# Seven products for the input duos alone, and the root on the output tiles

## The chip, the core and the metric

The kernel runs on one core of a Trainium2 chip. The metric is the time of one execution in microseconds (us) on the device. The engines are TensorE (PE; its weight loads are PEld), VectorE (DVE), ScalarE (ACT), GpSimd (POOL) and SyncE (SP, which issues most DMAs).

## What is computed

One layer of a hybrid encoder for 592 tokens (64 sample, 16 meta, 512 prompt) of width 1024: a feed-forward half-step, a combined projection with a state-space branch and an attention branch, their merge, and a second feed-forward half-step. The change concerns the two half-steps alone:

```python
def rmsnorm(x, g):
    xf = x.astype(jnp.float32)
    y = xf * lax.rsqrt(jnp.mean(xf * xf, axis=-1, keepdims=True) + EPS)
    return (y * g.astype(jnp.float32)).astype(x.dtype)

def swiglu(x, w_in, w_out):            # w_in 1024 x 5632, w_out 2816 x 1024
    a, b = jnp.split(x @ w_in, 2, axis=-1)
    return (jax.nn.silu(a) * b) @ w_out

h = h + 0.5 * swiglu(rmsnorm(h, norm_ffn1), ffn1_w_in, ffn1_w_out)
... the mixer ...
h = h + 0.5 * swiglu(rmsnorm(h, norm_ffn2), ffn2_w_in, ffn2_w_out)
```

## The kernel before

**Precision.** Every product of fp32 matrices is made of three matmuls in fp32r: each operand is split into a high part (rounded, an ACT copy) and a low part (the rest, a DVE subtraction), and high x high, low x high and high x low are summed in PSUM. So every weight tile costs ACT one pass and DVE one pass. `wh` and `wl` hold the parts of two slots of weights, 2048 elements per partition each; `raw` holds what the DMA brought, also two slots.

**Duos.** A feed-forward block (`ffn`, called with e = 0 and 1; 592 tokens, then 576) is a list of 38 duos, made by `duos_of`. An *input duo* makes one tile of 128 hidden features: two column tiles of w_in (a and b) times 1024 rows. An *output duo* adds two column tiles of 128 outputs to h. The 22 hidden tiles come in four parts of 6, 6, 6 and 4 (`PARTS`); in each part the input duos are followed by four output duos that sum over the part's tiles. Duo q uses PSUM banks 0 to 3 or 4 to 7 by turns.

**Seven products.** A duo is a product of a 2 x 2 block matrix of weights (two column tiles, two halves of the rows) and one of tokens (two halves of the rows, two halves of the tokens). A plain duo makes the eight block products, one half of the tokens in each matmul: 96 matmuls for an input duo. A *fast* duo (`fast`) makes seven by sums of blocks (Winograd's form of Strassen's product): 84 matmuls for input, 63 for an output duo of six tiles. Before, all input duos but the first of a block are fast and so are the twelve output duos of parts 0 to 2; the four output duos of the last part are plain, with 48 matmuls each.

**What a fast duo needs beside PE.** Four sums of weight blocks, all by POOL (`sum_for`, L904), written into `wl` in place of the low parts to come; six batches of high copies by ACT (`upper`, L1232) and six of low subtractions by DVE (`lower`, L1756), since the seven products need seven weight operands of 512 elements; four snapshots of partial sums from PSUM by ACT (`snap`, L1258); the sums of token blocks. The latter are made once per block for the input duos (`input_sums`, `input_upper`, `input_lower`), but for every hidden tile for the output duos (`first_difference`, the `late` tiles, `hidden_upper`, `hidden_lower`, L1270 to L1295, L1797 to L1820).

**Root.** The norm's root `rs` (one value per token) multiplies the a tile in `gate_a` (DVE) and, for b, the silu's result in two POOL operations (L952). In `gate_b` DVE adds and multiplies in four operations of half the tokens. After a fast output duo POOL adds two snapshots to h (L939, L944), and DVE adds the PSUM banks (`add_pair`).

**Order.** Every engine runs its instructions in the order of its list; the loops over duos interleave by hand what belongs to duo q, to the one before and to the one after. On ACT, for an input duo: snapshot 0, second hidden copy of the previous duo, weights of places 4 and then 0 of the next, snapshots 1 and 2, weights of places 1 to 5, silu, snapshot 3, first hidden copy (L1270 in the last part), last weights. In the first block the sum of squares (`square`, `gather`, `sum_squares`, `root`, `inverse`) runs beside duos 0 and 1, and the DMA of a slot is issued when `split_done` says that the slot's last low part is made.

## Time and profile before

| | us |
|---|---|
| median of 3 runs | 2122.32 (2121.72 to 2122.92) |
| profiled execution | 2123.01 |
| its span | 2121.3 |
| PE busy in it | 1930.2 (91%) |
| DVE, POOL, ACT busy | 1393.8, 1071.1, 1066.9 |
| first block, first matmul to last | 17 to 509 |
| second block | 1634 to 2103 |

Times in rows are us from the start of the span. Busy time of PE is a union of overlapping matmuls: a matmul's own duration (some 0.30 us) is longer than the distance to the next (0.14 us), so a stage is read by its length and the number of its matmuls. "PEclk" is the granted clock of PE, 1.00 being 2.4 GHz and 0.50 being 1.2 GHz. In a timeline "[1.62 <-DVE full]" is idle time of the engine before the row, and what ended it.

### The profile page before, as it was taken

What the parts mean: (1) busy time and instruction counts of PE and PEld (TensorE: products, weight loads), DVE (VectorE), ACT (ScalarE), POOL (GpSimd) and SP (SyncE); (2) the same over time, 40 slices, a digit from 0 to 9 for tenths busy, and PEclk for the clock granted to TensorE, in tenths of its full rate; (3) what the DMA queues carried; (4) which work ended last, traced back from release to release, by engine and by line L of the source; (5) the groups of instructions that cost most, each with busy time, mean ns of one, the idle gap of its engine ahead of it and who ended that gap; (6) DMA issues with size and microseconds to landing.
All of it is one profiled execution on the core that took longest, in us unless ns stands there. A gap on an engine that the chain in (4) does not pass through costs nothing. (4 is left out here: it accounts for less than half of the span.)

```text
span 2121.3 us, 37219 instructions
## 1 busy us (share of the span) xinstructions
PE 1930.2 (91%) x14087; PEld 1856.7 (88%) x14087; DVE 1393.8 (66%) x2151; ACT 1066.9 (50%) x2271; POOL 1071.1 (50%) x1024
## 2 busy tenths in 40 slices
PE   5788798889899999999999999999999789888787
PEld 4778798789799999999999999999999778888787
DVE  5898989877765356346635661224555898989874
ACT  5545545445565556555655664442224545545444
POOL 5578686852464345425432642232112578687760
PEclk9899999999899999999999999999999999999999
DMA  4212232224322412522161225234342113222222
GB/s 109 60 60 81 70 90 75 65 80 131 90 83 83 148 56 89 164 76 77 58 199 41 84 83 153 68 119 136 113 125 80 48 58 95 70 85 75 71 70 75
DMA packets 226959, 190.61 MB, mean 90 GB/s; under 512 B 11136, under 2 KB 215232, under 8 KB 225632
## 3 DMA queue, kind: packets, MB, share of 16 engines
q1 hardware_dynamic: 221824, 173.76, 26.9%
q0 software_dynamic: 4416, 14.32, 2.2%
q8 instruction: 112, 1.84, 0.4%
q14 instruction: 63, 0.52, 0.1%
q10 hardware_dynamic: 544, 0.17, 0.0%
HBM read 168.89 MB, written 19.33 MB: 89 GB/s over the span
## 5 line engine op out<-in xcount | busy, mean ns | idle before, releaser
L1040 POOL TENSOR_TENSOR wl<-raw,wh 128x512 fp32r<-128x512 f32 (+1 forms) x184 | 232.5, 1271 | 407.3 <-ACT wh L1163 406.9
L2189 PE MATMUL ps<-xah,wh 128*128 128x296 f32 (+1 forms) x1376 | 308.6, 306 | 11.9 <-DVE xal L1687 7.4
L2189 PE MATMUL ps<-xah,wl 128*128 128x296 f32 (+1 forms) x1376 | 307.8, 305 | 0.0
L2189 PE MATMUL ps<-xal,wh 128*128 128x296 f32 (+1 forms) x1376 | 302.3, 301 | 0.0
L1756 DVE TENSOR_TENSOR wl<-wl_plain,wh 128x512 fp32r<-128x512 f32 (+3 forms) x198 | 253.1, 1305 | 49.4 <-POOL wl_plain L904 26.7
L1232 ACT ACTIVATE wh<-wl_plain 128x512 fp32r<-128x512 f32 (+3 forms) x198 | 142.7, 721 | 196.3 <-POOL wl_plain L904 182.9
L2189 PEld LDWEIGHTS ps<-xah,wh 128*128 128x128 f32 x1376 | 223.0, 191 | 13.9 <-DVE xal L1687 6.4
L2189 PEld LDWEIGHTS ps<-xal,wh 128*128 128x128 f32 x1376 | 224.0, 190 | 0.0
L2189 PEld LDWEIGHTS ps<-xah,wl 128*128 128x128 f32 x1376 | 222.7, 190 | 0.1
L904 POOL TENSOR_TENSOR wl_plain<-raw 128x512 f32<-128x512 f32 (+1 forms) x132 | 187.1, 1425 | 12.6 <-PE ps L2256 12.0
L2256 PE MATMUL ps<-xth,wh 128*128 128x296 f32 (+1 forms) x504 | 156.3, 310 | 37.5 <-ACT act L1258 28.9
L2256 PE MATMUL ps<-xah,wh 128*128 128x296 f32 (+1 forms) x516 | 157.9, 306 | 33.0 <-ACT full L1258 17.8
L1756 DVE TENSOR_TENSOR wl<-raw,wh 128x512 fp32r<-128x512 f32 (+1 forms) x198 | 182.1, 937 | 0.2 <-DVE ss L1698 0.2
L952 POOL TENSOR_TENSOR act<-act,rs 128x296 f32<-128x296 f32 (+1 forms) x84 | 91.1, 1104 | 128.9 <-ACT act L1262 128.9
L2256 PE MATMUL ps<-xal,wh 128*128 128x296 f32 (+1 forms) x516 | 155.7, 302 | 0.0
L2256 PE MATMUL ps<-xah,wl 128*128 128x296 f32 (+1 forms) x516 | 155.6, 302 | 0.0
L2256 PE MATMUL ps<-xth,wl 128*128 128x296 f32 (+1 forms) x504 | 152.7, 303 | 0.0
L2256 PE MATMUL ps<-xtl,wh 128*128 128x296 f32 (+1 forms) x504 | 151.8, 301 | 0.0
L2256 PEld LDWEIGHTS ps<-xth,wh 128*128 128x128 f32 x504 | 97.7, 194 | 46.2 <-issue 35.7
L2256 PEld LDWEIGHTS ps<-xah,wh 128*128 128x128 f32 x516 | 99.6, 193 | 39.3 <-issue 29.6
L2201 PE MATMUL ps<-wh,xal 128*128 128x256 f32 (+1 forms) x440 | 128.0, 291 | 0.0
L2201 PE MATMUL ps<-wh,xah 128*128 128x256 f32 (+1 forms) x440 | 125.6, 286 | 1.1 <-ACT zr L1457 1.1
(394 smaller groups left out, 5559.5 us busy)
## 6 DMA issues: line engine op xcount, KB each, us to landing
raw<-in_ffn_w_in_dram SPq DMA_DIRECT2D x88, 512.0 KB, 5.1
raw<-in_w_in_dram SPq DMA_DIRECT2D x80, 512.0 KB, 4.5
raw<-in_ffn_w_out_dram SPq DMA_DIRECT2D x48, 384.0 KB, 3.7
brow<-acs_rows SPq DMA_DIRECT2D x8, 1184.0 KB, 6.7
raw<-in_w_br_ssm_dram SPq DMA_DIRECT2D x16, 512.0 KB, 3.9
bias<-bias_rows SPq DMA_DIRECT2D x32, 160.0 KB, 4.6
os_spill<-yT SPq DMA_DIRECT2D x8, 592.0 KB, 3.0
bias<-biasp_rows SPq DMA_DIRECT2D x16, 264.0 KB, 5.6
```

The source lines that it names most:

```text
L904: ins = pool.tensor_tensor(place(p, hk), a, b, op)
L952: pool.tensor_tensor(a, a, halfway(G["rs"][:, :], t, half), ALU.mult).then_inc(scaled_ready, 1)
L1040: ins = pool.tensor_tensor(wl[:, slot, k, 0:cols], raw[:, slot, k, 0:cols], wh[:, slot, k, 0:cols].bitcast(F32), ALU.subtract)
L1232: act.activation(places(wh, p, n, hk), src, ACT.Copy).then_inc(hi_ready if c == 5 else wh_part, 1)
L1756: dve.tensor_tensor(places(wl, p, n, hk), src, places(wh, p, n, hk).bitcast(F32), ALU.subtract)\
L2189: ins = pe.matmul(bank(b + a, half), w[:, slot, k, j * P:(j + 1) * P], x[:, k, a * half:(a + 1) * half], start=(k == 0 and w is wh and x i ...
L2201: ins = pe.matmul(bank(b, 256, m), x[:, k, t * P:t * P + m], w[:, slot, k, :], start=(k == 0 and w is wh and x is xh), stop=(k == KT - 1 a ...
L2256: ins = pe.matmul(bank(duo.b + b, half), weights_of(w, p, k), operand(duo, name, k, low), start=(start and k == 0 and w is wh and low == 0 ...
```

## The change

- `PRODUCTS` serve input duos alone. All output duos are plain (72 matmuls in parts 0 to 2, 48 in the last). In the first block two input duos are plain, in the second one (`PLAIN_IN`).
- The blocks of the rows are now every second row tile (tile 2k and tile 2k+1) instead of the lower and the upper four; T4 is a fourth tile in `xth` and `xtl` instead of overwriting x.
- Three of the four weight sums lie in a buffer of their own (`sums`), the fourth in `raw` in place. POOL makes the first and the one in place, DVE the two others (`sum_2`, `sum_4`). POOL's work in a block is these two sums per fast duo and no more; it starts them after the sum of squares is ready.
- The weights of a fast duo are split in three batches of 1024, 1536 and 1024 elements (`upper_x`, `upper_y`, `upper_z` and the same `lower_`), instead of six.
- An output duo's weights are one batch (`upper_plain`, `lower_plain`), at 0 or at 2560 in the row of `wh`.
- The root no longer multiplies b: `gate_b` is two operations on all tokens, POOL's two multiplications are gone, and the output tiles are multiplied by `rs` in `add_out`, ahead of the addition to h.
- Hidden tiles are kept as they are: one high copy, one low subtraction.
- The orders on ACT and DVE are new; in the second block the low halves of the token sums are made while w_out's product runs.

```diff
-PLAIN = len(PARTS) - 1
-HALF_IN, HALF_OUT = 4, 3
-FAST, FAST_OUTS = 33, 12
+PLAIN_IN = (2, 1)
@@ duos_of
-                fast = len(out) > 0 if into else part != PLAIN
+                fast = into and len(out) >= PLAIN_IN[ffn]
@@
-PRODUCTS = ((0, "B11", 3, True, 1), (1, "T1", 1, True, 2), (2, "T2", 3, False, 2), (3, "B22", 1, False, 3),
-            (4, "B21", 0, True, 4), (5, "T3", 3, False, 5), (6, "T4", 2, True, None))
+PRODUCTS = ((0, "B11", 3, True), (1, "B21", 0, True), (2, "T1", 1, True), (3, "T2", 3, False),
+            (4, "B22", 1, False), (5, "T3", 3, False), (6, "T4", 2, True))
@@ POOL: all of ffn (sums, additions into h, differences, multiplications by the root) becomes
+                pool.wait_ge(ss_ready, (1, 3)[e])
...
+                    pool.wait_ge(raw_ready[slot], raw_loads(duo, slots))
+                    pool.wait_ge(wl_part, 2 * duo.d)
+                    pool.tensor_tensor(G["sums"][:, 0, :].rearrange("p (k c) -> p k c", k=4), chunk(slot, 2, 1), chunk(slot, 2, 2), ALU.add)\
+                        .then_inc(s1_made, 1)
+                    pool.wait_ge(s2_made, duo.d + 1)
+                    pool.tensor_tensor(chunk(slot, 2, 1), chunk(slot, 1, 1), chunk(slot, 2, 1), ALU.subtract).then_inc(s3_made, 1)
@@ ACT, in the loop over duos
+                    if duo.fast:
+                        upper_z(duo)
+                        snap(duo, 0)
+                        if prev.into:
+                            hidden_upper(prev)
+                        if after.fast:
+                            upper_x(after)
+                        snap(duo, 1)
+                        if not after.fast:
+                            upper_plain(after)
+                        snap(duo, 2)
+                        if after.fast:
+                            upper_y(after)
+                        silu(duo)
+                        snap(duo, 3)
...
@@ DVE
+                def gate_b(duo):
+                    a, b = in_halves(actb[:, duo.s, :]), in_halves(full[:, duo.s, :])
+                    if duo.fast:
+                        dve.wait_ge(snap_ready, 4 * duo.d + 4)
+                        dve.wait_ge(prod_done, 7 * duo.d + 7)
+                        dve.tensor_tensor(b, halves(duo.b + 2, half=half), b, ALU.add).then_inc(c_done, 1)
+                        dve.wait_ge(c_done, duo.d + 1)
+                        dve.wait_ge(gated, duo.i + 1)
+                        dve.tensor_tensor(b, b, a, ALU.mult).then_inc(hid_made, 1)
...
+                def add_out(duo, u):
+
+                    hm, scaled = G["h"][:, 2 * duo.n + u, :], actb[:, u, :]
+                    dve.wait_ge(lin_out, unit_out(duo, u))
+                    link(dve.tensor_tensor(in_halves(scaled), halves(duo.b + 2 * u, half=half), rs, ALU.mult))
+                    dve.scalar_tensor_tensor(out=hm, in0=scaled, scalar=0.5, in1=hm, op0=ALU.mult, op1=ALU.add).then_inc(dve_free, 1)
...
+                    if duo.fast:
+                        if prev.into:
+                            gate_b(prev)
+                        lower_z(duo)
+                        if after.fast:
+                            sum_2(after)
+                        if prev.into:
+                            hidden_lower(prev)
+                        if after.fast:
+                            lower_x(after)
+                            sum_4(after)
+                        else:
+                            lower_plain(after)
+                        gate_a(duo)
+                        if after.fast:
+                            lower_y(after)
@@ DVE, opening of the first block
-                if m >= 4:
-                    input_sums(0, m - 4)
+                if m % 2:
+                    input_sums(0, m // 2)
+                if m in (4, 6):
+                    input_lower(0, m // 2 - 2)
@@ PE, in fast
+                        if p in (0, 2):
+                            pe.wait_ge(wl_part, 2 * duo.d + (1 if p == 0 else 2))
+                        if p == 5:
+                            duo_split()
...
+                        if not start:
+                            pe.wait_ge(snap_ready, 4 * duo.d + {3: 1, 4: 2, 5: 3}[p])
@@ PE
-            ffn(0, F1, (1, 1, 0), opening)
+            ffn(0, F1, (1, 0, 12, 0), opening)
...
-            ffn(1, G2, (0, 2, 4), closing=first_turns)
+            ffn(1, G2, (0, 1, 2, 4), closing=first_turns)
```

## Rows read from the trace of the kernel before

**Rows 1.** The page: busy time by engine, and the load of an input duo

```profile
PE 1930.2 (91%) x14087; PEld 1856.7 (88%) x14087; DVE 1393.8 (66%) x2151; ACT 1066.9 (50%) x2271; POOL 1071.1 (50%) x1024
...
raw<-in_ffn_w_in_dram SPq DMA_DIRECT2D x88, 512.0 KB, 5.1
```

**Rows 2.** Busy time by stage, the whole core (x is the number of instructions)

```profile
core 0: us, PE busy (x) PEld busy (x) DVE busy (x) ACT busy (x) POOL busy (x), PEclk, DMA share, GB/s
...
202.00:215.37 13.37, 11.95 (x87) 11.58 (x85) 12.14 (x15) 7.16 (x14) 9.63 (x8) 1.00 0.31 89
...
257.16:273.33 16.17, 10.76 (x66) 10.31 (x64) 14.66 (x19) 7.61 (x17) 11.66 (x11) 0.79 0.18 59
...
273.33:282.79 9.46, 8.81 (x66) 8.60 (x64) 7.57 (x9) 4.71 (x10) 8.56 (x8) 1.00 0.27 85
...
441.03:454.39 13.36, 11.69 (x86) 11.48 (x85) 11.11 (x14) 6.61 (x12) 7.62 (x7) 1.00 0.28 80
...
489.26:495.85 6.59, 6.59 (x51) 6.59 (x50) 4.66 (x6) 3.53 (x5) 0.00 (x0) 1.00 0.17 31
...
2082.66:2089.06 6.40, 6.40 (x51) 6.40 (x49) 3.32 (x4) 2.32 (x3) 0.00 (x0) 1.00 0.01 4
...
73.36:509.15 435.79, 378.50 (x2630) 366.99 (x2631) 378.79 (x429) 217.02 (x430) 302.48 (x238) 0.97 0.26 75
...
509.15:1634.01 1124.86, 1105.22 (x8363) 1058.95 (x8362) 563.56 (x1208) 570.23 (x1303) 423.04 (x487) 0.99 0.33 103
...
1669.94:2103.11 433.17, 370.32 (x2642) 358.48 (x2641) 374.24 (x422) 212.86 (x426) 297.84 (x238) 0.98 0.24 71
```

**Rows 3.** Waits of PE, 73 to 509 us: total us, times, longest

```profile
PE ps L2256 <- DVE wl L1756: 19.2, 22, 5.5
PE ps L2256 <- ACT full L1258: 17.2, 14, 1.4
PE ps L2256 <- DVE htl L1803: 14.1, 3, 4.7
PE ps L2256 <- ACT act L1258: 11.0, 8, 1.7
```

**Rows 4.** Timeline of DVE, one input duo: start us, us, instruction

```profile
447.02 0.68 DVE L1756 TENSOR_TENSOR wl<-wl_plain,wh 128x512 fp32r<-128x512 f32 x1
447.62 2.39 DVE L1756 TENSOR_TENSOR wl<-raw,wh 128x512 fp32r<-128x512 f32 x2
451.40 0.78 DVE L1769 TENSOR_TENSOR act<-ps,act 128x592 f32<-128x592 f32 x1 [1.39 <-PE ps L2256]
452.21 0.78 DVE L1770 TENSOR_TENSOR act<-act,rs 128x592 f32<-128x592 f32 x1
452.90 2.45 DVE L1756 TENSOR_TENSOR wl<-wl_plain,wh 128x1024 fp32r<-128x1024 f32 x2
```

**Rows 5.** Timeline of ACT in the same duo

```profile
444.51 0.70 ACT L1270 ACTIVATE hh<-full 128x592 fp32r<-128x592 f32 x1 [1.62 <-DVE full L1795]
...
445.63 0.40 ACT L1258 ACTIVATE act<-ps 128x296 f32<-128x296 f32 x1
...
449.56 1.06 ACT L1232 ACTIVATE wh<-wl_plain 128x1024 fp32r<-128x1024 f32 x1 [1.07 <-POOL wl_plain L904]
```

**Rows 6.** Timeline of POOL in the same duo

```profile
448.18 1.28 POOL L904 TENSOR_TENSOR wl_plain<-wl_plain,raw 128x512 f32<-128x512 f32 x1 [2.32 <-PE ps L2256]
...
453.79 2.24 POOL L952 TENSOR_TENSOR act<-act,rs 128x296 f32<-128x296 f32 x2 [2.63 <-ACT act L1262]
```

**Rows 7.** Timeline of DVE in the first block's opening

```profile
12.19 2.29 DVE L1675 TENSOR_TENSOR wl<-raw,wh 128x2048 fp32r<-128x2048 f32 x1 [12.19 <-POOL scanm L1004]
...
34.55 0.83 DVE L1687 SCALAR_TENSOR_TENSOR xal<-h,par,xah 128x592 fp32r<-128x592 f32 x1
...
49.17 6.92 DVE L1698 TENSOR_TENSOR ss<-ss,hh_plain 128x592 f32<-128x592 f32 x7
...
64.40 3.85 DVE L1707 RECIPROCAL rs<-rs 128x592 f32<-128x592 f32 x1 [4.36 <-ACT rs L1191]
```

More of the change, by code:

```diff
@@ L1234, in next_upper @@
[L1234 to L1252 removed]
+                actb, full, hh = G["act"], G["full"], G["hh"]
@@ new lines, in upper_x, with upper_y @@
+                def upper_x(duo):
+                    act.wait_ge(raw_ready[slots[duo.s]], raw_loads(duo, slots))
+                    act.wait_ge(*place_free(duo, duos, 1))
+                    act.activation(two_places(wh, 0), column(slots[duo.s], 1), ACT.Copy).then_inc(wh_part, 1)
+                def upper_y(duo):
+                    act.wait_ge(s4_made, duo.d + 1)
+                    act.wait_ge(*place_free(duo, duos, 4))
+                    act.activation(places(wh, 2, 3), G["sums"][:, :, :].rearrange("p s c -> p (s c)"), ACT.Copy).then_inc(wh_part, 1)
@@ L1306, in ffn @@
                 else:
-                    root(b)
-                    silu(duos[0])
-                act.wait_ge(lin_out, st.out.up(2))
-                for k in range(4):
-                    ins = act.activation(halfway(G["xh"][:, k, :], 2, half), G["xt4"][k], ACT.Copy)
-                ins.then_inc(xt_hi, 1)
-                for duo in duos[1:]:
-                    q, prev = duo.q, duos[duo.q - 1]
+                    input_upper(1, 3)
+                    upper_x(duos[1])
+                for duo in duos:
+                    q, prev = duo.q, duos[duo.q - 1] if duo.q else None
+                    after = duos[q + 1] if q + 1 < len(duos) else None
@@ L1759, in next_lower, with sum_2 @@
-                def next_lower(q, *cs):
-                    if q < len(duos) and duos[q].fast:
-                        for c in cs:
-                            lower(duos[q], c)
+                def sum_2(duo):
+                    dve.wait_ge(s1_made, duo.d + 1)
+                    dve.tensor_tensor(sums[:, 1, :].rearrange("p (k c) -> p k c", k=4), sums[:, 0, :].rearrange("p (k c) -> p k c", k=4),
+                                      chunk(slots[duo.s], 1, 1), ALU.subtract).then_inc(s2_made, 1)
@@ new lines, in ffn @@
+                    if duo.fast:
+                        fast(duo)
+                        continue
+                    duo_split()
+                    banks_free(duo)
+                    for u in range(2):
+                        m = 2 * duo.n + u
+                        if duo.into:
+                            sum_at = n_at if duo.q == q_at and u == u_at else None
+                            unit(0, u, xh, xl, KT, duo.b + 2 * u, tiles_after=xr() - KT if duo.q == u == 0 else None, at=duo.at,
+                                 between=opening if duo.q == u == 0 else lambda now: sum_squares(b) if now == sum_at else None)
+                            continue
+                        if m == KT - 1 and duo.part == len(PARTS) - 1 and closing is not None:
+                            closing()
+                        end = duos[duo.q - 1 - duo.n]
+                        if m == 0:
+                            pe.wait_ge(hid_ready, end.i)
+                        unit(0, u, hh, hl, duo.nt, duo.b + 2 * u, at=duo.at,
+                             before_last=(lambda: pe.wait_ge(hid_ready, end.i + 1)) if m == 0 else None)
```

730 lines of the change are left out of this document (263 added, 467 removed).

## The prediction

> **What bounds the kernel now.** I read the page first [rows 1]. TensorE (PE) is busy 91% of the span, so it looks like the bound; the table by stage [rows 2] says where it isn't. The middle of the kernel (509 to 1634 us) has PE busy 1105 of 1125 us, and the change doesn't touch it. The two feed-forward blocks are different: from the third input duo to the last output unit PE is busy 378.5 of 435.8 us in the first block and 370.3 of 433.2 us in the second, and ahead of these lie two openings of two duos each, 56 and 36 us long.
>
> A price per matmul comes next, because "busy" overlaps. The plain output duo at 489 us issues 48 matmuls in 6.59 us without a hole: 0.137 us each at 296 columns. The one at 2082 us gives 0.133 us at 288 columns [rows 2]. A fast input duo has 7 products x 4 row tiles x 3 = 84 matmuls, 11.5 us; it takes 13.37 us (202.00 to 215.37). A fast output duo has 63, 8.6 us; the ordinary one takes 9.46 us, but the first of a part takes 16.17 us at a mean clock of 0.79 [rows 2]. So some 1.8 us per input duo and 7.5 us per part are lost. The waits of PE [rows 3] name who ends them: in the first block 19.2 us VectorE's (DVE) low halves of the weights, 17.2 and 11.0 us ScalarE's (ACT) snapshots of a bank, 14.1 us DVE's low halves of the hidden tiles. The last has three waits, of up to 4.7 us: one per part, in the first output duo. (The longest of the first group, 5.5 us, ends the opening.)
>
> In a steady input duo I then followed ACT [rows 5]: hh waits 1.62 us for the gated product, and only behind it, at 445.63, comes the snapshot that frees bank 3; PE stands meanwhile. So it is the order on ACT, and DVE's speed behind it, and not ACT's own work.
>
> **The change, part by part.**
> 1. *PE work added.* Twelve output duos per block go from 63 to 72 matmuls: +108 per block. The first block also has one more plain input duo, 96 for 84: +12. Together 228, or 120 x 0.137 + 108 x 0.133 = +31 us. This lies on the bound; nothing hides it.
>
> 2. *Output duos.* Removed are the sums and snapshots for seven products, GpSimd's (POOL's) additions into h, and all prepared differences of hidden tiles. An output duo is now one high copy of 1536 on ACT, one low subtraction of 1536 on DVE and two additions that also multiply by the root. DVE prices from [rows 4]: 0.60 for 512 elements (447.02 to 447.62), 2.29 for 2048 [rows 7], so about 1.05 ns per element more: 1.14 for 1024, 1.68 for 1536, 0.69 for 592; an operation that reads PSUM 0.81 with its link (451.40 to 452.21), and 0.69 for the multiplication behind it. The duo costs DVE 1.68 + 2 x 1.5 = 4.7 us of PE's 9.86: hidden. Its first unit needs the last hidden tile only at its sixth row tile, 30 matmuls = 4.1 us in. Behind the last product come two gating operations (1.5), the high copy (0.70 [rows 5]) and the low one (0.69), 3.1 us with handovers: I charge nothing in parts 0 to 2 and 0.8 us in the last, where only 18 matmuls (2.5 us) lie before it. If the cover is gone, each part pays what the chain is longer than 4.1.
>
> 3. *Steady input duo.* I lay out one period, from the first matmul: products end at 1.8, 3.4, 5.1, 6.7, 8.3, 10.0 and 11.6. ACT: upper_z 0.2 to 1.3 (1.06 for 1024 [rows 5]), snapshot 2.3, hidden copy 3.0, upper_x 3.5 to 4.6, snapshot 5.5 (needed at 6.6), snapshot 7.2 (needed at 8.2), upper_y 8.4 to 9.9 (1536 at the same rate), silu 10.6, last snapshot 11.0. No snapshot stands behind a late wait any more. DVE: gate_b 1.50, lower_z 1.14, sum_2 0.60, hidden_lower 0.69, lower_x 1.14, sum_4 0.60, gate_a 1.50, lower_y 1.68: 8.85 us. POOL keeps two sums. What they cost DVE is seen in [rows 4, 6]: beside a POOL sum of 1.28 us two subtractions that should take 1.20 take 2.39, so 1.19 lost. The row at 452.90 (2.45 where 1.74 is due) loses 0.7 beside POOL's multiplications, which disappear. Two sums therefore lose 1.3 to 2.4, and DVE comes to 10.2 to 11.3 us, under PE's 11.5. Where a late gate_b holds hidden_upper on ACT, upper_x and the second snapshot are queued behind it, with some 2 us of slack. I take 11.6 us in the first block and 11.45 in the second (84 x 0.133 = 11.2): near PE's own price, with 0.1 to 0.25 for handovers. The low end is 11.5 and 11.2, the high end is the rival below.
> The Trainium skill (SBUF — State Buffer, section Who interferes with whom) says that such a pair holds an exclusive lock and the other fully blocks. The row at 447.62 agrees (1.19 of 1.28), the row at 452.90 shows less than that; by the rule DVE would be at the upper end of my bounds and the period another 0.3 us longer.
>
> 4. *Weights in DRAM.* The raw slot is released at lower_z, in the duo's own period, 3 to 4 us in; it was released in the period before. A load lands 5.1 us after its issue [rows 1], so some 9 us in, and the first sum wants it at 11.7: covered with 3 us.
>
> 5. *Openings.* First block: POOL makes one operation per token sum and DVE three, most of them ahead of the last low tile of x, which ends at 35.4 [rows 7]. Behind it DVE has one set of sums (1.7), the plain weights of duo 1 (2.2), two low halves of 1184 (2.6) and the squares' sums (6.9): these end near 48.7 instead of 56.1 [rows 7]. From there, by the prices above: sum matmuls and root 3 (an estimate), reciprocal 3.85 [rows 7], gate_a and silu of duo 0 1.5, gate_b, two sums and gate_a of duo 1 about 4, silu and hidden copy 1.4, upper_x and lower_x 2.3. The third duo can start at 64.5 instead of 73.36 [rows 2]: 9 us gained (5 to 13, since POOL starts its sums only behind the sum of squares, and a half clock can follow PE's stall). Second block: the tiles' low halves move under the w_out stage, and the third duo starts at 1662 instead of 1669.94: 8 us (4 to 10).
>
> 6. *Tails.* add_out is two operations for one, +0.7 us eight times, and behind it DVE has the mixer's low tiles. In the last part DVE was busy 4.7 of 6.6 us per duo [rows 2]; 1.5 more nearly fills it, and it ends a little behind PE. I charge 1.6 us for the first block and 0.7 for the second.
>
> **Sum.** First block from the third duo: 20 x 11.6 + 12 x 9.86 + 4 x 6.57 + 0.8 = 377.5 against 435.8, so 58.3, plus 9, less 1.6: 65.7 us. Second: 20 x 11.45 + 12 x 9.6 + 4 x 6.4 + 0.8 = 370.6 against 433.2, so 62.6, plus 8, less 0.7: 69.9 us. Together 135.6. The profiled execution took 2123.0 us (span 2121.3), the median of the runs is 2122.3, 0.7 less: 2122.3 - 135.6 = 1986.7, say 1987 us.
>
> **Rivals.**
> - *DVE becomes the bound.* It has 8.85 us of work, up to 2.8 lost to POOL, and eight handovers at 0.05 (an allowance; 0.03 lies between 452.18 and 452.21 [rows 4]): about 12.1 us. For: in this block DVE was busy 378.8 of 435.8 us, as much as PE [rows 2]. Against: in the last part it was busy 11.1 us beside four sums and two multiplications of POOL [rows 2]. 40 periods x 0.6 = +24: 2011 us.
> - *The handover to ACT stays* and a period remains 13.3 us (as the duo at 441 with its 13.36, where hidden tiles were plain already [rows 2]): only the output duos and the openings gain. 40 x 1.75 = +70: 2057 us. Against: the snapshot's place in ACT's order has changed.
> - *Slower.* The column reads of the new DVE operations step over every second row tile, a form that no row shows. If these (lower_x, lower_z, and the two sums) ran at twice their price, +3.5 us, DVE would need 8.85 + 3.5 + 2.8 + 0.5 = 15.6 us, and from a period of 11.5 + 135.6 / 40 = 14.9 us the kernel is slower than before: here 2151 us. Against: reads with a stride within a row tile (raw, 0.60 for 512) cost what the plain ones do.
> - *It doesn't do what it says*: the lower work on DVE and ACT is eaten by waits of the same length elsewhere, and the added matmuls cancel the rest. No row speaks for it; the output part is nearly free of handovers by its structure.
>
> **How the numbers follow.** Forecast (1968 to 2000) 0.52; DVE the bound (2000 to 2035) 0.25; ACT's handover stays 0.12; better than 1968 0.05; slower 0.04; no net effect 0.02. The range 1968 to 2035 leaves out about 0.2. Faster by over 0.2% 0.94, within 0.2% (4 us, about what a measurement can tell) 0.02, slower 0.04.
>
> **What would show it.** Right: input duos of 11.5 to 11.7 us without a gap over 0.3 us, output duos of 9.8 with no 4.7 us hole at a part's start and no drop of the granted clock in mid-block, the third duo near 64. Wrong: PE waiting for wl in front of the third product (DVE is the bound), for a snapshot in front of the fourth or fifth (ACT's order), or for the hidden tile in the sixth row tile of an output unit.

## The result and the profile after

| us | before | after |
|---|---|---|
| median of the runs beside each other | 2122.51 (4 runs) | 1981.53 (1978.73 to 1983.64, 4 runs) |
| profiled execution | 2123.01 | 1983.64 |
| its span | 2121.3 | 1982.0 |

After takes 0.9335 of the time of before (95% interval 0.9319 to 0.9352): 141 us less. The forecast was 1987 us.

The page of the kernel after, the same line as the first of [rows 1]:

```profile
PE 1919.9 (97%) x14315; PEld 1868.8 (94%) x14315; DVE 1206.0 (61%) x1869; ACT 947.3 (48%) x1807; POOL 559.3 (28%) x606
```

PE issues 228 matmuls more and is busy for 97% of a shorter span. DVE went from 1393.8 to 1206.0 us, POOL from 1071.1 to 559.3.

The waits of PE from 60 to 460 us (total us, times, longest), which answer to [rows 3]:

```profile
PE ps L2145 <- DVE wl L1654: 3.2, 1, 3.2
PE ps L2216 <- DVEq L1601: 2.2, 1, 2.2
PE ps L2093 <- ACT tx L1308: 1.3, 1, 1.3
PE ps L2081 <- DVE hl L1698: 0.8, 1, 0.8
PE ps L2081 <- DVE wl L1669: 0.3, 1, 0.3
```

62 us of waits in the first block have become one hole of 3.2 us ahead of the third duo and two of 0.8 and 0.3 us in the last part; the rows with L2216 and L2093 lie behind the block. No input duo of this block has a hole from the third on.

The table by stage, which answers to [rows 2]: two fast input duos (one in each block) and an output duo; then the first block's third duo; then the first block from its third duo, the middle, the second block from its third duo, and its opening.

```profile
core 0: us, PE busy (x) PEld busy (x) DVE busy (x) ACT busy (x) POOL busy (x), PEclk, DMA share, GB/s
172.99:184.45 11.46, 11.46 (x87) 11.46 (x85) 10.54 (x11) 6.57 (x9) 3.06 (x2) 1.00 0.34 93
...
228.66:238.50 9.84, 9.84 (x74) 9.84 (x73) 4.86 (x5) 1.49 (x1) 0.11 (x1) 1.00 0.37 108
...
1701.04:1712.18 11.14, 11.14 (x86) 11.14 (x85) 10.50 (x11) 6.52 (x9) 3.05 (x2) 1.00 0.35 94
62.08:76.34 14.26, 14.26 (x84) 14.26 (x85) 10.34 (x10) 6.32 (x9) 3.03 (x2) 0.79 0.27 75
62.08:440.18 378.10, 377.00 (x2736) 376.28 (x2736) 282.26 (x286) 158.27 (x208) 56.66 (x38) 0.99 0.29 85
440.18:1568.92 1128.74, 1105.94 (x8363) 1059.73 (x8363) 573.88 (x1220) 573.61 (x1307) 423.92 (x487) 0.99 0.33 104
1595.76:1962.60 366.84, 365.53 (x2750) 364.90 (x2749) 280.23 (x283) 156.49 (x208) 56.61 (x38) 1.00 0.28 84
1568.92:1595.76 26.84, 25.19 (x190) 24.91 (x189) 24.51 (x25) 13.96 (x17) 6.11 (x4) 1.00 0.15 40
```

A fast input duo takes 11.46 us with PE busy all the time (11.14 in the second block), where it took 13.37 [rows 2]. An ordinary output duo went from 9.46 to 9.84 us: its nine more matmuls cost 1.2 us (9 x 0.137), and the 0.8 us of waits that it had before are gone. The first of a part went from 16.17 to the same 9.84.

The account, from these windows and those of [rows 2]: first block from the third duo 435.8 to 378.1 (57.7 us less), its opening 73.36 to 62.08 (11.3 less), second block 433.2 to 366.8 (66.4 less), its opening 1669.94 - 1634.01 = 35.9 to 26.8 (9.1 less), the middle 1124.9 to 1128.7 (3.9 more), the end 18.2 to 19.4 (1.2 more). Sum 139.4 us, the difference of the two profiled executions. The medians differ by 1.6 us more, which is within the spread of the runs. No run keeps seven products in the output duos with the rest changed, so what the plain output duos give by themselves is read from these rows and not shown by an experiment.

How DVE fills a period is seen in its timeline from the gating of one duo to that of the next (start us, us, instruction, idle before it):

```profile
173.26 0.78 DVE L1687 TENSOR_TENSOR full<-ps,full 128x592 f32<-128x592 f32 x1
174.07 1.27 DVE L1690 TENSOR_TENSOR full<-full,act 128x592 f32<-128x592 f32 x1
175.27 1.21 DVE L1665 TENSOR_TENSOR wl<-raw,wh 128x1024 fp32r<-128x1024 f32 x1
176.41 0.68 DVE L1643 TENSOR_TENSOR sums<-sums,raw 128x512 f32<-128x512 f32 x1
177.01 0.76 DVE L1698 TENSOR_TENSOR hl<-full,hh 128x592 fp32r<-128x592 f32 x1
177.69 2.31 DVE L1654 TENSOR_TENSOR wl<-raw,wh 128x1024 fp32r<-128x1024 f32 x1
179.92 0.68 DVE L1648 TENSOR_TENSOR sums<-raw,sums 128x512 f32<-128x512 f32 x1
181.45 0.77 DVE L1676 TENSOR_TENSOR act<-ps,act 128x592 f32<-128x592 f32 x1 [0.85 <-PE ps L2145]
182.26 0.78 DVE L1677 TENSOR_TENSOR act<-act,rs 128x592 f32<-128x592 f32 x1
182.97 1.76 DVE L1659 TENSOR_TENSOR wl<-sums,wh 128x1536 fp32r<-128x1536 f32 x1
```

and POOL's in the same period:

```profile
173.41 1.30 POOL L908 TENSOR_TENSOR sums<-raw 128x512 f32<-128x512 f32 x1 [5.96 <-DVE wl L1659]
177.16 1.76 POOL L911 TENSOR_TENSOR raw<-raw 128x512 f32<-128x512 f32 x1 [2.45 <-DVE sums L1643]
```

The period runs from 173.26 to 184.72. Two gate_b (0.78, 1.27), lower_z 1.21, sum_2 0.68, hidden_lower 0.76, lower_x 2.31, sum_4 0.68, two gate_a (0.78 each), lower_y 1.76, and 0.85 us in which DVE waits for PE. The multiplication at 174.07 takes 1.27 where its like at 182.26 takes 0.78: it lies beside POOL's sum at 173.41. lower_x takes 2.31 where lower_z, of the same size, takes 1.21: it lies beside POOL's sum at 177.16.

### The profile page after: what moved, and what is told of

Same layout as the page of the kernel before. It is cut to its first block and busy times, and to the rows that moved or that the text cites. A ratio compares the mean times of both kernels' runs of the same rounds, so it can differ in the third digit from the quotient of the medians.

```text
span 1982.0 us, 35663 instructions
## 1 busy us (share of the span) xinstructions
PE 1919.9 (97%) x14315; PEld 1868.8 (94%) x14315; DVE 1206.0 (61%) x1869; ACT 947.3 (48%) x1807; POOL 559.3 (28%) x606
## 5 line engine op out<-in xcount | busy, mean ns | idle before, releaser
L2081 PE MATMUL ps<-xah,wh 128*128 128x296 f32 (+1 forms) x1696 | 377.7, 304 | 9.9 <-DVE xal L1586 5.8
L2081 PE MATMUL ps<-xah,wl 128*128 128x296 f32 (+1 forms) x1696 | 376.8, 304 | 0.0
L2081 PE MATMUL ps<-xal,wh 128*128 128x296 f32 (+1 forms) x1696 | 371.4, 301 | 0.0
L908 POOL TENSOR_TENSOR sums<-raw 128x512 f32<-128x512 f32 x41 | 53.0, 1294 | 415.6 <-DMA raw<-in_ffn_w_in_dram 214.6
L2093 PE MATMUL ps<-wh,xal 128*128 128x256 f32 (+1 forms) x440 | 128.0, 291 | 0.0
L2093 PE MATMUL ps<-wh,xah 128*128 128x256 f32 (+1 forms) x440 | 125.6, 286 | 1.2 <-ACT zr L1356 1.2
L2093 PE MATMUL ps<-wl,xah 128*128 128x256 f32 (+1 forms) x440 | 124.9, 284 | 0.0
L2145 PEld LDWEIGHTS ps<-xtl,wh 128*128 128x128 f32 x656 | 123.7, 189 | 0.0
L2145 PEld LDWEIGHTS ps<-xth,wl 128*128 128x128 f32 x656 | 123.6, 188 | 0.0
L911 POOL TENSOR_TENSOR raw<-raw 128x512 f32<-128x512 f32 x41 | 69.4, 1693 | 175.2 <-DVE sums L1643 175.2
L1101 ACT ACTIVATE wh<-raw 128x512 fp32r<-128x512 f32 (+1 forms) x192 | 110.4, 592 | 0.2
L1905 DVE SCALAR_TENSOR_TENSOR cvt<-xp,parh,cvt 128x595 f32<-128x595 f32 x96 | 98.7, 1029 | 18.9 <-ACT cvt L1421 17.0
```

Of the source, the lines that this page charges most:

```text
L908: pool.tensor_tensor(G["sums"][:, 0, :].rearrange("p (k c) -> p k c", k=4), chunk(slot, 2, 1), chunk(slot, 2, 2), ALU.add)\
L911: pool.tensor_tensor(chunk(slot, 2, 1), chunk(slot, 1, 1), chunk(slot, 2, 1), ALU.subtract).then_inc(s3_made, 1)
L1101: act.activation(wh[:, slot, k, 0:cols], raw[:, slot, k, 0:cols], ACT.Copy).then_inc(hi_ready if c == 3 else hi_part, 1)
L1905: ins = dve.scalar_tensor_tensor(out=c, in0=xp[:, j, tap:tap + CO], scalar=parh[:, bass.ds(conv_tile(i, g, j) + 32 * tap, 1)], in1=c, op0= ...
L2081: ins = pe.matmul(bank(b + a, half), as_row(w)[:, at + 256 * k + j * P:at + 256 * k + (j + 1) * P], x[:, k, a * half:(a + 1) * half], star ...
L2093: ins = pe.matmul(bank(b, 256, m), x[:, k, t * P:t * P + m], w[:, slot, k, :], start=(k == 0 and w is wh and x is xh), stop=(k == KT - 1 a ...
```

## The experiments

Two theories stood against each other, and the prediction had mixed them: PE's old holes came from the **order on ACT** (a snapshot of a bank queued behind a wait for DVE), or from **DVE's load**, which ACT's row only passes on. Two runs change the kernel before, three load one engine of the kernel after, and one gives it an order like the old one. Then come the parts of the change one by one, and at last what it left lying.

### The order of the snapshots, in the kernel before

before_snap: only the next duo's first snapshot moves ahead of ACT's hidden copy and last copy of weights.

```diff
                     if duo.fast:
-                        snap(duo, 0)
                         if q == 1:
+                            snap(duo, 0)
                             next_upper(1, 3)
...
                         snap(duo, 3)
+                        if after.fast and not (duo.into and not after.into):
+                            snap(after, 0)
+                            early = True
+                        else:
+                            early = False
                         if duo.into:
                             hidden_upper(duo, 0)
                         next_upper(q + 1, 5)
+                        if after.fast and not early:
+                            snap(after, 0)
```

> The kernel before, with one change: ACT frees the bank of the next duo's first snapshot ahead of its hidden copy and its last copy of weights, wherever the next duo is a fast one and no output duo follows an input duo. Order theory (PE's holes of before come from what stands ahead of a snapshot on ACT): the stall moves one snapshot on, since the fourth product wanted its bank only 1.3 us later, so little of it goes: 2112 to 2118 us. If the place of the first snapshot alone were the cause: 40 periods x 0.6 us less, 2097 us. If DVE's and POOL's load were the cause: 2122 us.

Measured 2121.58 us, 0.9994 of before [0.9984, 1.0003]: no difference, and not the 4 to 10 us of the order theory. The stall did move one snapshot on: in the first block PE's waits for an `act` snapshot went from 11.0 to 1.8 us, those for a `full` one from 17.2 to 21.9.

before_snaps: the second snapshot moves as well (`snap(after, 1)` behind `snap(after, 0)`, and none in its old place).

> As the last, with the first and the second snapshot of the next duo both ahead of ACT's hidden copy and last copy of weights. Order theory: the waits of PE on ACT (some 25 us in the first block, 38 in the second) go, and DVE, busy 12.1 to 13.0 us of a period of 13.3, bounds next at about 12.5: 2095 to 2100 us. If DVE's and POOL's load set the period and ACT only passes it on: 2118 to 2123 us.

Measured 2112.98 us, 0.9953 [0.9937, 0.9970]: 9.5 us under the 2122.51 of the table above, not 22 to 27. One steady period, as a row of its table by stage (columns as above):

```profile
186.30:199.70 13.40, 11.96 (x85) 11.46 (x85) 13.10 (x15) 7.51 (x15) 9.41 (x7) 1.00 0.26 72
```

and PE's waits in the first block:

```profile
PE ps L2265 <- DVE wl L1765: 26.5, 32, 5.5
PE ps L2265 <- DVE htl L1812: 14.1, 3, 4.7
PE ps L2265 <- ACT act L1258: 10.6, 20, 0.6
```

The waits for a `full` snapshot (17.2 us in [rows 3]) are gone, those for weights' low halves rose from 19.2 to 26.5, and the period is 13.40 us, no shorter than before. DVE is busy 13.10 of these 13.40 us. In the kernel before it was busy 12.14 of 13.37 [rows 2]. Of the rise, 1.1 us is one pair of subtractions, here in before and then in before_snaps:

```profile
210.12 1.28 DVE L1756 TENSOR_TENSOR wl<-raw,wh 128x512 fp32r<-128x512 f32 x2
```

```profile
197.10 2.38 DVE L1765 TENSOR_TENSOR wl<-raw,wh 128x512 fp32r<-128x512 f32 x2
```

In before, POOL's sum began inside the pair, at 210.74, and POOL's own operation got longer (1.82 us); in before_snaps it began ahead of the pair, at 196.70, and DVE's got longer. So the order on ACT was one limit, at 13.3 us, and DVE's load, with what it loses to POOL, a second, right behind it, at 13.4. Mending the first alone gave 9.5 us. 5.3 of them come from the last part's four input duos, which took 50.4 and 49.6 us from first matmul to first matmul instead of 53.0 and 52.3: hidden tiles are plain there, and DVE has less to do. "ACT full" in the list of waits was the link that closed last, and taking it away showed DVE.

### An order like the old one, in the kernel after

```diff
                         upper_z(duo)
-                        snap(duo, 0)
                         if prev.into:
                             hidden_upper(prev)
                         if after.fast:
                             upper_x(after)
+                        snap(duo, 0)
                         snap(duo, 1)
```

> The kernel after, with ACT's first snapshot of a fast input duo put back behind its hidden copy (which waits for DVE's gated product) and behind upper_x: the order in which the kernel before had it. If ACT's order was the cause of the old period of 13.3 us: that stall is back, 12.5 to 13.3 us per duo, 2020 to 2055 us. If DVE's load was (the run with both snapshots early showed DVE idle for only 0.19 us of a period of 13.4): DVE has the gated product ready by 3 us into the duo, ACT ends upper_x at 4.6, the snapshot lands near 5.0 where the fourth product wants its bank at 5.1 to 5.3, and the kernel takes 1982 to 1990 us.

Measured 1987.64 us (1986.27 to 1987.78), 0.9363 [0.9347, 0.9378]: about 6 us more than after. A period of it:

```profile
158.55:170.14 11.59, 11.59 (x86) 11.47 (x85) 10.52 (x11) 6.46 (x9) 3.04 (x2) 1.00 0.33 92
```

11.59 us instead of 11.45, and in the second block 11.34 instead of 11.15: the fourth product starts a little late, 16 times in each block, 2.2 and 3.1 us, and the duo ahead of the third in the second block has a new hole of 1.16 us for a snapshot. With the lighter DVE this order costs some 6 us of the 141 (the terms above add up to 6.5). The two tests of the order, from either side, say 6 and 9.5 us.

### More work on DVE

dve_1: lower_x is made twice.

```diff
+                    if duo.q > 2:
+                        link(dve.tensor_tensor(two_places(wl, 0), column(slots[duo.s], 1), two_places(wh, 0).bitcast(F32), ALU.subtract))
                     dve.tensor_tensor(two_places(wl, 0), column(slots[duo.s], 1), two_places(wh, 0).bitcast(F32), ALU.subtract)...
```

> The kernel after, with one low half of the weights (lower_x, 1024 columns) made twice in every fast input duo from the fourth duo on: DVE +1.16 us per duo, 10.5 + 1.16 = 11.7 us against PE's 11.45. Slack theory (DVE has 0.85 us idle in a period, and some 2 us of lead that an output duo refills): 1983 to 1990 us, say 1986. If every us on DVE beyond its idle time shows at once: 38 periods x 0.3 to 0.4 us, 1995 to 1998 us. If DVE has more slack than its timeline shows: 1982 us.

Measured 1981.74 us (1981.33 to 1982.04): as after (1981.53), and under the 1983 to 1990 of the slack theory. The two operations in DVE's timeline:

```profile
175.95 2.30 DVE L1655 TENSOR_TENSOR wl<-raw,wh 128x1024 fp32r<-128x1024 f32 x1
178.29 1.22 DVE L1656 TENSOR_TENSOR wl<-raw,wh 128x1024 fp32r<-128x1024 f32 x1
```

Only the first lies beside POOL's sum; the second costs 1.15 us from start to start of the next. DVE then has no idle time left, and its period is 11.90 us (lower_z begins at 173.53 and at 185.43) against PE's 11.45. It falls behind by 0.45 us per duo, and over a part of six duos that stays within the lead that it regains in the output duos. In the second block, where PE's duo takes 11.15 us, it doesn't quite: four duos at the ends of the first three parts take 11.42 to 11.87 us, 1.7 us together. Two unrelated differences hide this in the total: the third duo of the first block lost 1.2 us less to the half clock, and started 1.0 us earlier.

dve_2: lower_x and lower_y are both made twice.

> The kernel after, with lower_x (1024 columns) and lower_y (1536) made twice in every fast input duo from the fourth duo on: DVE 10.6 + 1.2 + 1.76 = 13.5 us, so a period of 13.4 to 13.6, 2 us over PE's. DVE's load theory: each duo from the fourth on is 2.0 us longer less a lead of some 2.1 us that each part's output duos give back: 37 x 2.0 - 7 x 2.1 = 59 us, 2035 to 2050 us. If DVE's load does not matter beside ACT's order: under 2000 us.

Measured 2040.07 us, 0.9611 [0.9594, 0.9627]: 58.5 us more than after, 59 expected. A period:

```profile
189.89:203.58 13.69, 11.98 (x87) 11.50 (x85) 13.49 (x13) 6.01 (x10) 3.04 (x2) 1.00 0.28 77
```

and PE's waits in the first block:

```profile
PE ps L2150 <- DVE wl L1664: 14.2, 12, 1.2
PE ps L2150 <- ACT full L1194: 5.5, 11, 0.5
```

DVE is busy 13.49 of 13.69 us. And here is the signature of [rows 3] again: waits for weights' low halves, and beside them eleven waits "ACT full". ACT's work and order were not touched in this run. The second snapshot stands behind the hidden copy, which waits for DVE's gated product; a late DVE so shows up under ACT's name.

### More work on ACT

```diff
+                    if duo.q > 2:
+                        for _ in range(2):
+                            link(act.activation(two_places(wh, 0), column(slots[duo.s], 1), ACT.Copy))
                     act.activation(two_places(wh, 0), column(slots[duo.s], 1), ACT.Copy).then_inc(wh_part, 1)
```

> The kernel after, with ACT's copy upper_x made three times in every fast input duo from the fourth duo on: ACT +2.1 us per duo (6.6 to 8.7 us of 11.45, far from full), all of it ahead of the second snapshot. Order theory (what stands ahead of a snapshot on ACT is what counts, not ACT's load): the second snapshot comes 0.35 to 0.4 us late for the fifth product in each duo, 38 x 0.37 = +14 us, 1996 us (1988 to 2005). If ACT's load decides: 1982 us, as it is busy only 76% of the period.

Measured 2005.31 us (2004.42 to 2007.44), 0.9451 [0.9435, 0.9467]: 24 us more than after, more than the 14 expected. PE's timeline at such a stall:

```profile
180.49 0.30 PE L2148 MATMUL ps<-xth,wl 128*128 128x296 f32 x1
181.20 0.40 PE L2148 MATMUL ps<-xah,wh 128*128 128x296 f32 x1 [0.41 <-ACT full L1197]
181.44 0.30 PE L2148 MATMUL ps<-xal,wh 128*128 128x296 f32 x1
```

The hole has the 0.41 us of the expectation (nearly every duo of the first block that has a fast one behind it shows this number), yet these duos take 12.12 to 12.14 us, 0.68 more; in the second block a hole of 0.52 makes 0.79. From start to start the stall takes 0.71 us, where 0.137 is the pace, and the matmul behind it 0.24: the first matmul after a stop runs 0.40 us instead of 0.30, and the gap of the list starts only at the modelled end of the last one. There are 16 such duos in each block, one of them 1.7 us longer: 16 x 0.68 + 15 x 0.79 + 1.7 = 24.4 us. ACT was busy 8.5 of 12.1 us there. What stands ahead of a snapshot decides, not ACT's load.

### Who makes the weight sums

sums_pool: all four by POOL. sums_dve: all four by DVE, and POOL does nothing in the blocks.

```diff
 POOL (sums_pool)
                     pool.tensor_tensor(G["sums"][:, 0, :]..., chunk(slot, 2, 1), chunk(slot, 2, 2), ALU.add)...
+...
+                    pool.tensor_tensor(s[1], s[0], chunk(slot, 1, 1), ALU.subtract).then_inc(s2_made, 1)
                     pool.wait_ge(s2_made, duo.d + 1)
+                    pool.tensor_tensor(s[2], chunk(slot, 1, 2), s[1], ALU.subtract).then_inc(s4_made, 1)
                     pool.tensor_tensor(chunk(slot, 2, 1), chunk(slot, 1, 1), chunk(slot, 2, 1), ALU.subtract)
 DVE (sums_pool): sum_2 and sum_4 do nothing
 DVE (sums_dve): sum_2 makes sums 0 and 1, sum_4 makes sum 2 and the one in place; POOL's loop is taken out
```

> All four weight sums of a fast duo by POOL, as before the change; the rest as changed. Theory (PE's own price bounds the input duo, DVE has about 0.9 us to spare): DVE gives up two operations of 0.60 and is slowed by two more POOL sums, 0.55 to 1.15 each, so its 10.5 us per duo become 10.4 to 11.6 and the period stays 11.45 to 11.6 us; time 1981 to 1988 us, say 1983. Rival (the split of the sums carries a good part of the gain): a period of 12.2 us or more, 2010 us.

> All four weight sums by DVE, POOL idle in the feed-forward blocks. Theory: DVE has 1.2 us more of its own and loses nothing to POOL (1.7 us now: 0.55 beside the first sum, 1.15 beside the one in place), so its busy time per duo falls from 10.54 to 10.0 us and the time doesn't change: 1981.5, within 3. Every two-input DVE operation should show its undisturbed length (lower_x 1.21 instead of 2.31). Rival (POOL's help is needed): DVE at 11.7 us per duo, period 11.8, time 1996.

Measured 1977.24 us (1976.57 to 1978.35) with POOL's four, less than the 1981 to 1988 expected, and 1983.54 us (1982.28 to 1984.49) with DVE's four; after, with two and two, lies between. None of them changes an input duo, 11.45 us in the first block in all three: the 4 us that sums_pool gains lie around the openings, where its third duo starts at 60.44 instead of 62.08 and fewer matmuls follow at half clock, and where the second block's opening is 25.5 us instead of 26.8. Of the first, 1.2 us are the half clock (the third duo took 13.08 instead of 14.26 us), which the last section warns of. DVE in sums_pool:

```profile
170.44 0.77 DVE L1687 TENSOR_TENSOR full<-ps,full 128x592 f32<-128x592 f32 x1
...
172.47 2.31 DVE L1665 TENSOR_TENSOR wl<-raw,wh 128x1024 fp32r<-128x1024 f32 x1
174.70 1.86 DVE L1698 TENSOR_TENSOR hl<-full,hh 128x592 fp32r<-128x592 f32 x1
176.49 2.31 DVE L1654 TENSOR_TENSOR wl<-raw,wh 128x1024 fp32r<-128x1024 f32 x1
```

and POOL:

```profile
170.62 1.30 POOL L908 TENSOR_TENSOR sums<-raw 128x512 f32<-128x512 f32 x1 [4.39 <-DVE wl L1659]
172.00 1.70 POOL L912 TENSOR_TENSOR sums<-sums,raw 128x512 f32<-128x512 f32 x1
173.78 2.16 POOL L914 TENSOR_TENSOR sums<-raw,sums 128x512 f32<-128x512 f32 x1
175.89 1.82 POOL L915 TENSOR_TENSOR raw<-raw 128x512 f32<-128x512 f32 x1
```

The two sums that DVE no longer makes (1.36 us) come back as longer operations beside POOL's: hidden_lower takes 1.86 us instead of 0.76 and lower_z 2.31 instead of 1.21. In sums_dve, with no POOL operation beside it, lower_x takes 1.22 us and the multiplication of gate_b 0.77, as expected, and DVE is busy 10.23 us of a period. DVE has no idle time in this period. The addition that reads PSUM (170.44) is not held up by the sum at 170.62, which lasts longer than it and begins 0.18 us into it.

### The root

root_b: DVE multiplies b by the root in gate_b (one operation more per input duo), and an addition into h is one operation again.

```diff
                         dve.wait_ge(c_done, duo.d + 1)
+                        link(dve.tensor_tensor(b, b, rs, ALU.mult))
                         dve.wait_ge(gated, duo.i + 1)
...
@@ add_out
+...
-                    link(dve.tensor_tensor(in_halves(scaled), halves(duo.b + 2 * u, half=half), rs, ALU.mult))
-                    dve.scalar_tensor_tensor(out=hm, in0=scaled, scalar=0.5, in1=hm, op0=ALU.mult, op1=ALU.add)
+                    dve.scalar_tensor_tensor(out=hm, in0=halves(duo.b + 2 * u, half=half), scalar=0.5, in1=hm, op0=ALU.mult, op1=ALU.add)
```

> The root back on b, by DVE in gate_b, and not on the output tiles. Theory: one DVE operation more per input duo (0.7, to 11.25 of 11.45 us) and one less per output unit; nothing changes in mid-block and the tails shorten by up to 4 us: 1978 us. Rival (the root's place on the outputs is what keeps DVE from being the bound): period 11.8 us, 1993.

Measured 1980.31 us (1979.71 to 1980.39): 1.2 us under after, whose own runs span 5 us. The tail between the blocks is 4.9 us shorter (from the first block's last matmul at 440.75 to the second's first at 1564.57 are 1123.8 us, after 1128.7). Some is lost elsewhere: 24 output duos of 9.91 and 9.67 us instead of 9.84 and 9.60 are 1.7 us, PE's hole ahead of the last hidden tile is 1.63 and 1.62 us instead of 0.83 and 1.18, the second block's opening is 27.6 us instead of 26.8, and three input duos behind it take 11.40 instead of 11.15. Putting the root on the output tiles was no gain by itself.

both_undone: all four sums on POOL, and the root on b by two multiplications of POOL behind silu, as before, with one operation per tile in add_out. What is left of the change are the seven products for input duos alone, the plain output duos and hidden tiles, the new orders and the openings.

```diff
+                    if duo.into:
+                        pool.wait_ge(gated, duo.i + 1)
+                        for t in (2, 1):
+                            a = halfway(G["act"][:, duo.s, :], t, G["half"])
+                            ins = pool.tensor_tensor(a, a, halfway(G["rs"][:, :], t, G["half"]), ALU.mult)
+                        ins.then_inc(scaled_ready, 1)
...
@@ DVE, gate_b
-                        dve.wait_ge(gated, duo.i + 1)
+                        dve.wait_ge(scaled_ready, duo.i + 1)
```

> Four sums by POOL and the root on b by two POOL multiplications behind the silu, as before: of the change there stay the plain output duos, the three batches and the orders. Theory: gate_b waits for POOL until some 1.5 us into the next duo, and DVE loses 0.7 to 1.2 us more beside POOL: DVE needs about 11.9 us, +0.45 in 40 periods, less some 4 us of the tails: 1996 us (1985 to 2010). So nine tenths of the gain stay. Rival (POOL's load was the cause): most of the gain in the input duos goes, a period of 13.3 us, 2050.

Measured 1999.92 us (1998.4 to 2002.12), 0.9419 [0.9403, 0.9434]: 122.6 us under before, 18.4 over after. A period from lower_z to lower_z, and DVE's wait in it:

```profile
182.28:195.05 12.77, 12.50 (x92) 12.25 (x91) 11.84 (x10) 6.01 (x9) 9.22 (x7) 1.00 0.30 83
```

```profile
193.36 1.76 DVE L1698 TENSOR_TENSOR full<-full,act 128x592 f32<-128x592 f32 x1 [0.90 <-POOL act L922]
```

DVE is busy 11.8 of 12.8 us and waits 0.90 for POOL's multiplication: POOL is now in the chain, and the sums that it makes beside DVE's work cost DVE 1.1 us each in lower_z, hidden_lower and lower_x. So 87% of the gain stays without these two edits, of which the title names one, the root; they are worth 18 us together, and sums_pool shows that it isn't the sums alone. With the root off POOL, all four sums can be there without a cost.

### What was left lying

opening: upper_x and lower_x of the first block's third duo ahead of the root, the two sums of the first fast duo ahead of the reciprocal in both blocks, and upper_y and lower_y ahead of the hidden copies.

```diff
@@ ACT: upper_x(duos[2]) ahead of the loop, upper_y(after) ahead of hidden_upper(prev)
@@ DVE, ahead of the loop over the duos
+                    lower_x(duos[2])
...
+                first = duos[1] if last else duos[2]
+                sum_2(first)
+                sum_4(first)
@@ DVE, a plain input duo
-                        if after.fast:
-                            sum_2(after)
-                            sum_4(after)
                         gate_a(duo)
-                        if q:
-                            hidden_lower(prev)
-                            if after.fast:
-                                lower_x(after)
                         if after.fast:
                             lower_y(after)
+                        if q:
+                            hidden_lower(prev)
```

> The kernel after, with the two openings reordered: upper_x and lower_x of the third duo ahead of the root in the first block, the two sums of the first fast duo ahead of the reciprocal in both blocks, upper_y and lower_y ahead of the hidden copies. Theory: PE's hole of 3.2 us ahead of the third duo and the stretch at half clock behind it (2.8 us) go in part, and 1 us of the 1.65 us hole in the second block: 5 to 6 us less, 1974 to 1977 us. If the reciprocal and squares of DVE bound the opening whatever stands around them: 1981 us.

Measured 1976.70 us (1975.47 to 1977.17), 4.8 us under after. The third duo in its table by stage:

```profile
59.07:71.37 12.30, 11.79 (x86) 11.52 (x85) 10.16 (x10) 7.64 (x10) 3.44 (x2) 1.00 0.32 87
```

The hole of 3.2 us ahead of the third duo has shrunk to 0.5 us inside it, the third duo starts at 59.07 instead of 62.08, and it takes 12.30 us at the full clock instead of 14.26 at 0.79.

best_pool: this opening, four sums on POOL, and the root on b in the last part of each block alone.

> The last kernel's opening, all four sums on POOL, and in the last part of each block the root put on b by DVE, so that an addition into h is one operation there. Theory: the openings' gain (5 us, of which the sums on POOL give 4 already) and 3 us at the two tails: 1970 to 1973 us. If the tails' gain is lost again because DVE is full in the last input duos: 1975 to 1977 us.

Measured 1973.16 us (1971.58 to 1973.98), 0.9296 [0.9280, 0.9311]: 8.4 us under after, and the fastest of all. The last low tile of the first block on DVE:

```profile
436.67 0.83 DVE L1589 SCALAR_TENSOR_TENSOR xul<-h,par,xuh 128x592 fp32r<-128x592 f32 x1
```

The middle (434.51 to 1558.00) takes 1123.5 us instead of 1128.7. This low tile begins 2.2 us behind PE's last matmul (434.51); its like in after begins 5.7 us behind.

## Why the prediction was right, step by step

The median came out 5.5 us under the forecast of 1987 and well in the range; 139.4 us by the profiled executions against 135.6 of the sum. (Three small slips in its working: the terms of the first block add up to 377.4 and not 377.5, those of its opening to 64.8 and not 64.5, and the rival "DVE becomes the bound" puts up to 2.8 us on POOL where part 3 has 1.3 to 2.4. None changes the forecast by more than 0.3 us.)

1. **PE's added work.** Right, and the price per matmul held: 84 matmuls in 11.46 us are 0.136, in 11.14 us 0.133.

2. **Output duos.** Right: 9.84 us (9.86 forecast), DVE busy 4.86 of it (4.7), no hole in parts 0 to 2. The first output duo of the last part has a hole of 0.83 us in the first block (0.8 charged) and of 1.18 in the second.

3. **The steady input duo.** The mechanism was right and DVE's size too: 10.54 us busy, forecast 10.2 to 11.3, of which POOL's two sums take 0.49 + 1.10 = 1.6 (1.3 to 2.4). What was too high is the allowance for handovers on PE, 0.1 to 0.25 us per duo: there are none, a period is 84 matmuls and nothing else. In the second block this made 20 x 0.3 = 6 us. 2.3 us of it went into the last part's output duos (28.7 instead of 26.4 us; 1.5 of them are ten matmuls of the closing, L2175, between the last two tiles, which the sum left out), so that block came to 366.8 instead of 370.6. In the first the allowance was 3.0 us too high, and the half clock of the third duo cost 2.8 that the sum didn't have: that 378.1 stands so near 377.5 is luck.
The contention with POOL stands in the rows above, and its size can be read from them: an operation loses what is left of the other engine's at its start, less 0.14 us. The multiplication starts at 174.07 with 0.64 us of POOL's sum left (173.41 + 1.30) and loses 0.49; lower_x starts at 177.69 with 1.23 left and loses 1.10; in sums_pool lower_z, hidden_lower and lower_x start with 1.22 to 1.24 left and lose 1.10 each. It holds the other way too: POOL's sum at 172.00 starts with 0.55 us of DVE's multiplication left and takes 1.70 instead of 1.29. An addition with one operand in PSUM loses nothing.
The Trainium skill (SBUF — State Buffer, section Who interferes with whom) calls the pair of ports that DVE and POOL share an exclusive lock, and says that a DVE instruction with two SBUF inputs contends with a POOL instruction that reads SBUF, and one with at most one SBUF input (outside its two-port modes) doesn't. This trace agrees with all three, to within that 0.14 us. The prediction read the lock as the loss of a whole POOL operation, 1.2 us for each of the two sums; only the rest of it is lost, so the two cost 1.6 us and not 2.4.

4. **Weights in DRAM.** Right as far as the trace goes: no wait of PE, ACT or DVE for a load shows up in an input duo of the first block.

5. **Openings.** The sum of squares ended at 47.9 us (48.7 forecast), the third duo started at 62.08 (64.5) and then lost 2.8 us to the half clock, for 11.3 - 2.8 = 8.5 us net against 9. The second block gained 9.1 against 8. (In the kernel before the third duo ran at a mean clock of 0.84, so part of that loss isn't new.) The run with the reordered opening shows what both left over: 4.8 us.

6. **Tails.** The term was mis-sized: 3.9 us in the middle instead of 1.6, and 1.2 at the end instead of 0.7. The prediction let DVE end "a little behind PE"; it ends 6.6 us behind. The timeline's row of the last low tile, and the row of the table by stage for the last output duo:

```profile
445.92 0.83 DVE L1586 SCALAR_TENSOR_TENSOR xul<-h,par,xuh 128x592 fp32r<-128x592 f32 x1
```

```profile
433.36:440.18 6.82, 6.82 (x48) 6.58 (x48) 6.32 (x10) 3.18 (x5) 0.00 (x0) 1.00 0.48 154
```

This low tile (first row) ends at 446.75, PE's last matmul at 440.18. [rows 2] give DVE 4.66 us busy in an output duo of 6.59 in the last part, and the prediction added 1.5 to that. But this is the second of the four duos; the work behind the additions (a low tile and a square's sum for each tile, and the weights' low half) gathers in the last two. In after the last output duo of the first block has DVE busy 6.32 of 6.82 us, with a low half of weights, and two tiles' additions and squares are still to come when PE ends. root_b and best_pool, with one addition per tile, show middles of 1123.8 and 1123.5 us, so the whole 3.9 us, and a little more, hangs on that one operation per tile. On PE it shows as two holes, of 2.2 us at 447.54 and 1.3 us at 455.70 (L2216 and L2093 in the list of waits above); before, root_b and best_pool have neither.

**What was wrong in the reading of before.** The prediction said of the old holes "it is the order on ACT, and DVE's speed behind it". The time came out right because the change mended both; as a diagnosis it was half a truth. The order alone was worth 9.5 us in the old kernel (before_snaps) and 6 in the new (snap_late). The rest of the gain in the input duos came from DVE's load: between before_snaps and after its operations in a period went from 13.73 us (weights 7.28, gates 4.08, hidden tiles 2.37) to 11.01 (weights 5.28, sums 1.36, gates 3.61, hidden tile 0.76). The rival "ACT's handover stays" would have fallen with the right diagnosis, since the order was not what held the period; the rival "DVE becomes the bound" was the near one. How near, the two runs with more work on DVE tell: 1.15 us more per duo cost 1.7 us in all, 2.9 us more cost 58.5 us. The edge lies some 1.2 us above the kernel after: 0.85 us idle and a share of the lead that output duos give back.

The rival "slower" needed strided reads at twice the price. lower_x and lower_z read every second row tile. lower_z takes 1.21 us, 1.14 from its start to the next (1.14 forecast), and sums take 0.68 for 512 elements, as the subtractions did before: no such effect.

## What to carry to other kernels

A wait under one engine's name is only the last link. Before crediting a fix to it, add up what the engine behind it does in a period, and what it would lose to a third engine once its operations move: here DVE showed 12.1 of 13.4 us busy, which promised over 1 us per period for a new order, and with that order it was busy 13.1 and gave none. Then the work has to go. Saving multiplications on the bounding engine is no gain where it costs the helpers more than they have: this kernel issues 228 matmuls more and is 141 us faster. And a small operation added to a chain at a stage's end (here 0.8 us per tile) should be costed against the engine's load in the stage's last stretch and not against its mean load: it cost 4 us, and undoing it in the last part alone, with the openings reordered and the sums on POOL, gives 8 us more.

## What the runs showed of the hardware beyond this

- **A stall costs more than its hole.** A listed idle time of 0.41 us made the duo 0.68 us longer (act_2); 0.27 us go to the first matmuls behind a stop, and to the modelled end of the one before it.
- **The clock after a hole isn't the same every time.** Ahead of the third duo of the first block after, dve_1, dve_2, act_2 and snap_late have the same hole of 3.2 us. In the first 4 us behind it the mean granted clock was 0.50 in after (the lower of the two levels throughout, with 0.74 in the next 4 us), 0.57 in act_2, 0.64 in dve_1, 0.68 in dve_2, and 1.00 in snap_late, where it did not fall at all. A hole of 1.9 us (sums_pool) and one of 4.0 us (root_b) were both followed by 0.57, one of 4.5 us (sums_dve) by 0.50. The third duo took 14.26 us in after, 13.06 in dve_1 and 11.69 in snap_late, though neither of the two edits reaches the work ahead of that duo. Differences of 1 to 3 us between kernels with such a hole are therefore not to be read as effects of an edit; opening and best_pool, with holes of at most 0.5 us there, kept 1.00.
